# A transformer kernel whose first weights are loaded ahead of the norm's vectors, with the norm's gain and bias moved behind the transpose

## The reference

```python
def _layer_norm(x, g, b):
    mu = jnp.mean(x, axis=-1, keepdims=True)
    var = jnp.mean(jnp.square(x - mu), axis=-1, keepdims=True)
    return (x - mu) * lax.rsqrt(var + LN_EPS) * g + b

x = _layer_norm(x, ln_in_g, ln_in_b)
for l in range(DEPTH):
    mix = _mixer(x, w_in[l], b_f[l], w_pa[l], w_pb[l], w_pc[l], w_o[l])
    x = _layer_norm(DN_ALPHA * x + mix, ln1_g[l], ln1_b[l])
    ffn = _swiglu(x, w_gate[l], w_up[l], w_down[l])
    x = _layer_norm(DN_ALPHA * x + ffn, ln2_g[l], ln2_b[l])
```

## Time and profile before

| | |
|---|---|
| time, median of 3 runs | 873.25 us (873.02 to 873.25) |
| profiled execution | 873.52 us, of which the span is 871.7 us |
| TensorE busy (PE) | 840.5 us, 96% of the span |
| VectorE (DVE) | 513.3 us, 59% |
| ScalarE (ACT) | 400.1 us, 46% |
| GpSimd (POOL) | 56.7 us, 7% |
| bytes by DMA | 149.35 MB, mean 171 GB/s |
| first transpose on TensorE | 11.64 us |
| first weight pass on TensorE | 17.40 us |

### The profile page before, as it was taken

How to read it: one execution, slowest core, us unless ns; L and a number is a source line. 1 busy time by engine, 2 the same in 40 slices (tenths; PEclk the granted TensorE clock), 3 DMA queues, 4 the chain that set the end, 5 groups by cost and what they waited for, 6 DMA issues and landing times.

```text
span 871.7 us, 10732 instructions
## 1 busy us (share of the span) xinstructions
PE 840.5 (96%) x4216; PEld 695.9 (80%) x4216; DVE 513.3 (59%) x728; ACT 400.1 (46%) x536; POOL 56.7 (7%) x86
## 2 busy tenths in 40 slices
PE   3999999999999999999999999999999899999995
PEld 2888888888877888888878889888888688888884
DVE  7565564556796545445685656463778764555436
ACT  3476465543344344444336655554443453344430
POOL 0012331000000000000000324200000000000000
PEclk9999999999999999999999999999999999999998
DMA  9574433457636765664436443435654576656501
GB/s 324 160 257 164 133 119 116 141 181 229 193 104 244 232 194 183 193 203 149 154 108 225 144 159 106 142 103 181 243 177 144 192 246 203 189 183 193 193 0 49
DMA packets 93458, 149.35 MB, mean 171 GB/s; under 512 B 3424, under 2 KB 52832, under 8 KB 93408
## 3 DMA queue, kind: packets, MB, share of 16 engines
q1 hardware_dynamic: 93408, 148.66, 52.5%
HBM read 147.60 MB, written 1.05 MB: 171 GB/s over the span
## 4 chain that ended last, share of the span: by engine, by line
PE 92%; DVE 5%; DMA 1%; ACT 0%; issue 0%; SPq 0%; DVEq 0%
PE bank L1044 82%; PE bank L1059 3%; PE bank L1103 3%; PE bank L1135 2%; DVE w_lo L860 2%; PE bank L1123 1%; PE bank L1069 1%; DMA raw<-in_w_in 1%; DVE stats L977 1%; DVE x L1010 1%; DVE x L974 1%; DVE x L1007 1%; DVE act_lo L865 0%; DVE newton L994 0%; DVE rstd L999 0%
## 5 line engine op out<-in xcount | busy, mean ns | idle before, releaser
L860 DVE TENSOR_TENSOR w_lo<-raw,w_hi 128x2048 fp32r<-128x2048 f32 (+3 forms) x142 | 309.0, 2180 | 91.5 <-ACT w_hi L762 91.0
L1044 PE MATMUL bank<-w_hi,act_hi 128*128 128x512 f32 (+2 forms) x864 | 342.8, 397 | 3.3 <-DVE act_lo L865 3.3
L1044 PE MATMUL bank<-w_hi,act_lo 128*128 128x512 f32 (+2 forms) x864 | 333.3, 386 | 0.0
L1044 PE MATMUL bank<-w_lo,act_hi 128*128 128x512 f32 (+2 forms) x864 | 332.2, 384 | 0.0
L762 ACT CAST w_hi<-raw 128x2048 fp32r<-128x2048 f32 (+3 forms) x142 | 257.2, 1813 | 125.5 <-PE bank L1044 100.4
L1044 PEld LDWEIGHTS bank<-w_hi,act_hi 128*128 128x128 f32 x864 | 163.2, 189 | 33.2 <-DVE act_lo L865 3.7
L1044 PEld LDWEIGHTS bank<-w_hi,act_lo 128*128 128x128 f32 x864 | 162.8, 188 | 33.0
L1044 PEld LDWEIGHTS bank<-w_lo,act_hi 128*128 128x128 f32 x864 | 163.4, 189 | 28.8
L1044 PE MATMUL bank<-w_hi,y_hi 128*128 128x512 f32 x240 | 95.2, 397 | 0.0
L1044 PE MATMUL bank<-w_hi,y_lo 128*128 128x512 f32 x240 | 93.7, 390 | 0.0
L1044 PE MATMUL bank<-w_lo,y_hi 128*128 128x512 f32 x240 | 93.5, 390 | 0.0
(11 more groups left out here) (88 smaller groups left out, 551.3 us busy)
## 6 DMA issues: line engine op xcount, KB each, us to landing
raw<-in_w_in SPq DMA_DIRECT2D x48, 1024.0 KB, 5.2
raw<-in_w_gate SPq DMA_DIRECT2D x44, 512.0 KB, 4.0
raw<-in_w_up SPq DMA_DIRECT2D x44, 512.0 KB, 5.0
raw<-in_w_down SPq DMA_DIRECT2D x22, 1024.0 KB, 4.9
raw<-in_w_o SPq DMA_DIRECT2D x8, 1024.0 KB, 5.2
raw<-in_w_in SPq DMA_DIRECT2D x4, 768.0 KB, 4.4
raw<-in_w_pa SPq DMA_DIRECT2D x4, 768.0 KB, 4.4
raw<-in_w_pc SPq DMA_DIRECT2D x4, 768.0 KB, 4.4
```

Source lines behind the costliest of these rows:

```text
L860: dve.tensor_tensor(weights(w_lo, i, HI_SLOTS), weights(raw, i, RAW_SLOTS), weights(w_hi, i, HI_SLOTS).bitcast(F32), ALU.subtract).then_in ...
L1044: ins = pe.matmul(bank[use[0]][:, 0:width], a, w[:, k, c0:c0 + width], start=start and k == 0 and p == 0, stop=stop and k == nk - 1 and p ...
```

## The change

It concerns the input norm and the first pieces of layer 0.

- **Loads.** SyncE issues x, then piece 0, then the 64 KB identity and a new 8 KB array with gain and bias as columns (`norm_cols`, 128 x 2 x 8), then two more pieces. The broadcast rows of gain and bias are loaded behind the fifth piece, and the three table transfers (528, 131 and 6 KB) behind the seventh piece instead of the third.
- **Quarters.** The former piece 0 is two pieces of 128 x 1024 (two k blocks each) that share one slot. Pieces are so counted one higher from there on. The low part of the second quarter is made by GpSimd, not by VectorE.
- **Norm.** VectorE only computes (x - mean) * rstd, one operation per half, with no gain. The turn transposes that; then ScalarE applies gain and bias, which are now one value per partition: four operations of 128x128 from the bank into a part of `merged`, and the cast to act_hi and the subtraction to act_lo read it there. x for the residual gets its gain and bias later (step "affine"): two VectorE operations of 128x1024 per tile, behind column block 1 in the plan.
- **Idle passes.** TensorE starts with 48 matmuls of zeros (256 columns, into a bank that isn't in use), and does 16 more behind the first turn.
- **Order.** In layer 0 column block 0 is done for both tiles, then block 1. Splits of pieces 3 to 5 are planned behind block 0 of tile 0.

Everything else, the rest of layer 0 and layer 1, stays.

```diff
+ACT_SLOTS = [[0, 1, 2, 3], [4, 5, 6, 7]]
 HELD = 3
+WARM = (48, 16)
...
+        if layer == 0 and c == 0:
+            for quarter in range(2):
+                piece(("qkv", 0, 0, quarter), [(rows(w["w_in"], 2 * quarter, 2, c0, width), 0, width)], 2, width)
+        for half in range(layer == 0 and c == 0, 2):
             piece(("qkv", c, half), [(rows(w["w_in"], 4 * half, 4, c0, width), 0, width)], 4, width)
...
     statistics({t: None for t in range(TT)}, 1)
     scale(0)
     split_hi()
     split_lo()
-    turn_x(0, 0, 1)
     split_hi()
     split_lo()
+    plan.append(("warm", WARM[0]))
+    turn_x(0, 0)
+    plan.append(("warm", WARM[1]))
     scale(1)
-    for _ in range(HI_SLOTS - 2):
-        split_hi()
+    split_hi()
+    split_lo()
+    turn_x(0, 1)
 
     staged = [0]
     events = []
...
+        if layer == 0:
             for c in range(2):
...
+                for t in range(TT):
+                    if (c, t) == (0, 1):
+                        for _ in range(HI_SLOTS - 2):
+                            split_hi()
+                    use0 = bank(2 * c + t)
+                    for half in range(2):
+                        if (c, t, half) == (0, 0, 1):
+                            turn_x(1, 0, 1)
+                        qkv(c, t, (half,), use0, t == TT - 1, False)
+                    if c == 1:
+                        plan.append(("affine", t, turned[t, 1]))
...
-            sp.dma_start(tables[:, 0:P], d["tables"][:, 0:P]).then_inc(ident_loaded, 16)
-            load_gain_bias(0)
...
+                    if i == 1:
+                        sp.dma_start(tables[:, 0:P], d["tables"][:, 0:P]).then_inc(ident_loaded, 16)
+                        sp.dma_start(norm_cols[:, :, :].rearrange("p a k -> p (a k)"), d["norms"]
+                                     ).then_inc(norms_loaded, 16)
...
-                    if i == 2:
+                    if i == 4:
+                        load_gain_bias(0)
+                    if i == 6:
...
+            pool.wait_ge(hi_done, 2)
+            pool.tensor_tensor(weights(w_lo, 1, HI_SLOTS), weights(raw, 1, RAW_SLOTS),
+                               weights(w_hi, 1, HI_SLOTS).bitcast(F32), ALU.subtract).then_inc(lo_on_pool, 1)
...
+                    source_rows = bank[b]
+                    if src == "first":
+                        if idx == 1:
+                            act.wait_ge(norms_loaded, 16)
+                        source_rows = first_rows[dk // 4]
+                        if t:
+                            act.wait_ge(drained[first_use[dk][0]], first_use[dk][1])
+                        first_use[dk] = (b, n)
+                        for k in range(nk):
+                            ins = act.activation(source_rows[:, k * P:(k + 1) * P], bank[b][:, k * P:(k + 1) * P],
+                                                 ACT.Identity, bias=norm_cols[:, 1, dk + k:dk + k + 1],
+                                                 scale=norm_cols[:, 0, dk + k:dk + k + 1])
+                        link(ins)
                     act.copy(hi[dst][:, dk:dk + nk, t * P:(t + 1) * P],
-                             group_view(bank[b], nk, P)).then_inc(turn_hi, 1)
+                             group_view(source_rows, nk, P)).then_inc(turn_hi, 1)
...
-                if kind == "lo":
+                if kind == "lo" and step[1] != 1:
...
+                elif kind == "affine":
+                    _, t, (b, n) = step
+                    dve.wait_ge(gb_loaded, 32)
+                    dve.wait_ge(filled[b], n)
+                    link(dve.tensor_tensor(x[t][:, :], x[t][:, :], gain_bias[:, 0, :], ALU.mult))
+                    link(dve.tensor_tensor(x[t][:, :], x[t][:, :], gain_bias[:, 1, :], ALU.add))
+                elif kind == "scale" and step[2] <= TT:
+                    _, t, idx = step
+                    for nh in range(2):
+                        xh = x[t][:, nh * NW:(nh + 1) * NW]
+                        dve.tensor_scalar(xh, xh, mean_var[:, t, 0:1], rstd[:, t:t + 1], ALU.subtract,
+                                          ALU.mult).then_inc(x_ready, 1)
...
-            pe.wait_ge(ident_loaded, 16)
+            pe.wait_ge(logf_zeroed, 2)
             for step in PLAN:
                 kind = step[0]
+                if kind == "warm":
+                    for _ in range(step[1]):
+                        pe.matmul(bank[4][:, 0:SEQ], logf_hi[:, 0, :], logf_lo[:, :, :].rearrange("p t n -> p (t n)"),
+                                  start=True, stop=True)
+                    if step[1] == WARM[0]:
+                        pe.wait_ge(ident_loaded, 16)
                 if kind == "mm":
```

More of the change, by code:

```diff
@@ L328, in qkv @@
             for half in halves:
-                mm(at[("qkv", c, half)], t, ("act", 4 * half), [(use, 0, QKV[c][1], half == 0, half == 1)],
-                   frees, turned[t, half], (use,) if half else ())
+                if (layer, c, half) == (0, 0, 0):
+                    for quarter in range(2):
+                        mm(at[("qkv", 0, 0, quarter)], t, ("act", [2 * quarter, 2 * quarter + 1]),
+                           [(use, 0, QKV[0][1], quarter == 0, False)], frees, turned[t, 0])
+                else:
+                    mm(at[("qkv", c, half)], t, ("act", ACT_SLOTS[half]),
+                       [(use, 0, QKV[c][1], half == 0, half == 1)], frees, turned[t, half], (use,) if half else ())
                 if tick_too and not (half == 1):
@@ L430, in gate_up @@
         def gate_up(c, t, half, use, frees):
[L431 removed]
+            mm(at[("gu", c, half)], t, ("act", ACT_SLOTS[half]), [(use, 0, NW, half == 0, half == 1)],
                frees, turned[t, half], (use,) if half else ())
@@ L546, in trunk @@
         tables = sb("tables", [P, TABLE_COLS])
+        norm_cols = sb("norm_cols", [P, 2, KT])
+        first_rows = [merged[1][:, j * NW:(j + 1) * NW] for j in range(2)]
         cum_row = sb("cum_row", [P, SEQ], F32R)
@@ L864, in _ @@
                     dve.wait_ge(turn_hi, idx)
-                    dve.tensor_tensor(lo[dst][:, dk:dk + nk, t * P:(t + 1) * P], group_view(bank[b], nk, P),
+                    full = group_view(first_rows[dk // 4] if src == "first" else bank[b], nk, P)
+                    dve.tensor_tensor(lo[dst][:, dk:dk + nk, t * P:(t + 1) * P], full,
                                       hi[dst][:, dk:dk + nk, t * P:(t + 1) * P].bitcast(F32),
@@ L1181 @@
     arrays["in_tables"] = constant_tables()
+    arrays["in_norms"] = np.ascontiguousarray(np.concatenate(
+        [np.asarray(inputs[name]).reshape(KT, P).T for name in ("ln_in_g", "ln_in_b")], axis=1))
     for name, a in arrays.items():
```

82 lines of the change are left out of this document (44 added, 38 removed).

## The result

The changed kernel takes **876.06 us** (median of 10 runs, 873.80 to 879.22); the kernel before, beside it on the same chip, 873.42 (10 runs, 873.02 to 874.09). The ratio is 1.0032, with a 95% interval of 1.0020 to 1.0044: 0.3% slower, where 870.3 was forecast, and above the forecast's range of 867.2 to 873.4. The profiled execution took 878.12 us, span 876.3, one of the slower ones; where it matters, its times are read against a second profile of the same kernel (after_again, span 872.2). Of the before kernel the profiled execution took 873.52, span 871.7.

A forecast was written before the change was run, and what follows sets the result against it. TensorE's weight passes were taken as the bound from 17.40 us, with VectorE's chain then allowing the forget sum at 54.9. Gain 57.8 - 54.9 = 2.9, so 873.25 - 2.9 = 870.3 us; range 867.2 to 873.4.

The forecast's parts named there:

- From 17.40 TensorE's weight passes hold it, almost unbroken.: Chain of waits in the kernel before: TensorE's weight passes bound it from 17.40 us on.
- The rest of the kernel is the same and shifts with it: Everything behind the forget gate's sum moves along unchanged; sum at 54.9 instead of 57.8, so 2.9 us gained.
- Scaling at 9.95, GpSimd beside it.: Input norm: VectorE's first scaling starts at 9.95 and runs beside GpSimd's low part, which starts at 9.65.
- GpSimd's piece gets in front of the scaling: Rival, chance 0.24: GpSimd holds the scaling until 12.25, x comes 2.3 later, gain falls to 0.6: 872.6 us.
- Piece 7 lands 5.9 after its issue.: Weight transfer of piece 7: issued by SyncE at 28.6, lands 5.9 us later at 34.5.
- the tables blocking SyncE's issue: Rival, chance 0.11: table transfers ahead of piece 7 delay its issue by 4.1 us, giving 874.5 us.
- VectorE: 15.3 from the cast to the forget step, 3.1 to logf_lo.: VectorE behind piece 7's cast: 15.6 us of work less 0.3 to the forget gate at 51.8, sum possible 3.1 later.
- ScalarE's turn 2.1: ScalarE per half tile: four gain-and-bias ACTIVATEs taken as 1.5 us, plus a cast of 0.59, 2.1 instead of 0.59.
- Scaling 0.69 each: VectorE's scaling of x: one operation of 128x512 per half, taken as 0.69 us.
- GpSimd 1.2 to 2.6: GpSimd's low part of the second quarter: at most 2.6 us, with 1.21, half the VectorE split, as floor.
- Split 3 from 24.0: VectorE's split of piece 3 runs from 24.0 to 26.3, 0.8 us before TensorE wants it at 27.1.
- This rival has no time of its own: Rival of idle passes failing to keep the clock fast: costs 0.3 us, covered by the new forget-gate wait; no separate time.

The follow-up runs named there:

- before_idle_passes: The kernel before with idle passes on TensorE alone, 72 at the start and 26 behind the first tile's transposes: 873.42 us, ratio 0.9999.
- low_on_vector: The changed kernel with the low part of the second quarter on VectorE instead of GpSimd: 873.86 us, ratio 1.0004.
- low_and_gate: low_on_vector with 26 idle passes of 256 columns on TensorE in its wait for the forget sum: 873.66 us, ratio 1.0005.
- tables_mid: low_on_vector with the three table transfers issued behind piece 5 instead of behind piece 6: 872.16 us, ratio 0.9989.
- low_and_affine: low_on_vector with both tiles' affine moved ahead of the split of piece 7, into VectorE's idle stretch: 871.38 us, repeated 871.29.
- gate_passes: The changed kernel with 26 idle passes of 256 columns on TensorE ahead of its wait for log f: 876.37 us, ratio 1.0038.
- sum_ahead: low_and_affine with layer 0's cumulative sums ahead of a cast on ScalarE and ahead of a split on VectorE: 871.41 us.
- affine_behind_gate: The changed kernel with both tiles' affine on VectorE behind the forget step instead of ahead of it: 878.63 us, ratio 1.0067.
- no_idle_passes: The changed kernel without its 48 and 16 idle passes: 876.89 us, ratio 1.0048.
- tables_late: low_on_vector with the three table transfers issued behind piece 7 instead of behind piece 6: 872.89 us, ratio 0.9995.
- gpsimd_behind_scaling: The changed kernel with one more wait: GpSimd starts its low part only after VectorE has scaled the first tile: 874.50 us, ratio 1.0015.
- after: The first profile of the changed kernel, unedited; that execution took 878.12 us, span 876.3.
- all_three: sum_ahead with the three table transfers behind piece 7: 872.77 us.
- low_affine_tables: low_and_affine with the three table transfers behind piece 5: 871.46 us.

## Why the prediction was wrong

One relation of the profiles settles most of it. From the end of logf_lo on VectorE to the first scores on TensorE (times and span are of the profiled execution, the median is of all runs):

| kernel | logf_lo ends | scores start | block of 24 | span | median |
|---|---|---|---|---|---|
| before | 56.16 | 61.09 | 69.15 | 871.7 | 873.42 |
| before_idle_passes | 55.98 | 60.90 | 68.95 | 871.5 | 873.42 |
| changed | 59.14 | 65.37 | 73.45 | 876.3 | 876.06 |
| changed, second profile | 56.37 | 61.40 | 69.49 | 872.2 | 876.21 |
| low_on_vector | 56.19 | 61.10 | 69.18 | 872.0 | 873.86 |
| low_and_gate | 55.83 | 60.76 | 68.84 | 871.7 | 873.66 |
| tables_mid | 54.13 | 59.06 | 68.69 | 871.4 | 872.16 |
| low_and_affine | 53.82 | 58.75 | 66.83 | 869.6 | 871.38 |

Scores start 4.9 to 5.0 behind logf_lo in every row but one (the changed kernel's first profile, 6.2, where the clock was slow for twelve passes), whether TensorE waits or not; the block of 24 follows 8.1 later (9.6 in tables_mid, where the twelve passes behind the scores took 4.43); the span ends 802.5 to 802.9 behind that. The kernel before is on this line too. What fills the 4.9 is the cast, the split and the row in the chain of gate_passes above. Off the line are kernels that change what lies between: sum_ahead, with the row ahead of cast and split, 3.5, and affine_behind_gate, with four more operations there, 8.4; and no_idle_passes, 6.6, where TensorE was last.

Now the steps, in the order of the prediction.

- *"From 17.40 TensorE's weight passes hold it, almost unbroken."* **This failed first.** In before the row of sums ended at 60.95 and the scores started at 61.09, 0.14 later. In low_and_gate, where TensorE demonstrably waits for the row, the distance is the same 0.14 (60.62 to 60.76). So at this place TensorE had no slack to give: its passes and the row came in together, and the chain of waits named only TensorE. before_idle_passes took 2.5 us off TensorE's first 24 passes and gained nothing. I had looked for the next tight place, found 1.65 of slack at the sum, and stopped there; the next one, 3 us further, had none.
- *"The rest of the kernel is the same and shifts with it"*, the gain of 2.9 read at the sum. By the relation above logf_lo at 54.9 gives 54.9 - 56.16 = -1.3, so even with each other number right the time would have been 872, not 870.3. That the sum itself moved 2.9 was of no use.
- *Scaling at 9.95, GpSimd beside it.* The rival "GpSimd's piece gets in front of the scaling" (0.24) happened, with its 2.3 (12.20 instead of 9.95), but not in every execution. Its price in the median is 2.35 (876.21 to 873.86). I had the rule, and drew from it the wrong order: I let VectorE's scaling start 0.3 behind GpSimd and run. Even 128x1 operations with two tensor inputs were held, 2.41 for 0.23. What the Trainium skill says (SBUF — State Buffer, SBUF: two separate sides), that whoever starts first has the shared ports for its whole instruction and the other fully blocks, fits all three profiles: the held operation ended 0.09, 1.08 and 0.55 behind the end of GpSimd's (12.08, 13.23 and 14.36).
- *Piece 7 lands 5.9 after its issue.* It took 7.24 (6.6 to 7.5 in the other profiles with this order of transfers, 8.3 in no_idle_passes). It went out behind the tables; tables_mid shows the same piece 5.1 after the split that lets it go (28.82 to 33.97), and 1.7 less time. The rival had the tables blocking SyncE's issue; they took 0.51, 0.43 and 0.43. It was the bytes.
- *VectorE: 15.3 from the cast to the forget step, 3.1 to logf_lo.* Cast at 38.98, its end 40.9, forget at 56.04: 15.1, and 3.1. Right, as was the cause, the affine in that chain: moving it into the idle time gains 2.5 (873.86 to 871.3). I had named 34.5 as the landing of a piece that VectorE waits for and did not ask what else could stand there.
- *ScalarE's turn 2.1*: 1.51 + 0.62. *Scaling 0.69 each*: 0.50. *GpSimd 1.2 to 2.6*: 2.34. *Split 3 from 24.0*: 24.34 in low_on_vector, with the first weight pass at 14.25 for 14.2. So the beginning was right but for GpSimd, in part by luck: VectorE makes both quarters there and ends at 13.23, where I had GpSimd and then VectorE end at 13.46. In the changed kernel it stood at 27.19, 3.2 late: 2.25 is the hold, and with x late TensorE had been idle for 3.0, so the 16 idle passes ran at half clock (3.18) in front of the second transposes.
- *"This rival has no time of its own"* (the idle passes and the clock): right for the median, as gate_passes and low_and_gate show, and wrong for the slowest group: the clock fell in the new wait, which I had not thought of. There it cost 65.4 - 64.1 = 1.3.

Together: 870.3, plus 1.6 for reading the gain at the sum instead of at the scores, plus 1.3 for logf_lo at 56.2 instead of 54.9 without GpSimd in the way (low_on_vector; nearly all of it piece 7's transfer), plus 2.35 for GpSimd, make 875.55, of 876.06. 0.2 of the rest is the kernel before itself, 873.42 here and 873.25 there.

Open is why the quarters land about 1 us earlier in some executions than in others, which sets the order of GpSimd and VectorE, and what parts the upper groups of times. Not tried is to give GpSimd a share of the work where VectorE idles, at 35 to 40.9.

## What to carry to other kernels

A chain of waits names who came last, not by how much: before pricing a gain on it, write down the second arrival at each of the next meeting points, and take the smallest slack as the most that can be gained by speeding up the one named. An in-order engine that waits for a transfer is the place for work that nobody waits for; the same four operations cost 2.5 us behind that wait, and in front of it 1.15 of VectorE's wait was still left. A transfer that is moved needs an idle stretch of the DMA, since between two pieces of a serial chain its bytes are on the path.

## What the runs showed of the hardware

- When a GpSimd subtraction of 128x1024 begins close to a VectorE operation, the order of the two can differ from one execution to the next: GpSimd at 9.74 and the scaling held to 12.20 in one profile, the scaling at 9.98 and GpSimd at 10.67 in the other. The times of this one program lay in three groups, 0.6% apart: 873.8 to 875.0, 876.0 to 876.9, 877.9 to 879.6. One more wait (gpsimd_behind_scaling) made it 874.1 to 875.9.
- The hold reached operations of one column: 2.41 us for a pair that takes 0.23. The GpSimd subtraction took 2.34 when it was first, and 3.23 when VectorE's quarter was.
- TensorE idle for 3.0 us came back at a granted clock of 0.50, at once or within 1.5 us, and had 1.00 again 3 to 6 us after its return (after, after_again, low_on_vector); 26 idle passes in that wait kept it at 1.00. The length of the idle stretch alone does not decide: 3.2 us of it in all_three were followed by 1.00 throughout, and after a wait of 1.4 the clock stayed at 1.00 in low_and_affine and fell to 0.50 in tables_mid and low_affine_tables. In no_idle_passes a wait of 1.7 us was followed by 0.50 from 46 to 58 us.
- The record of the granted clock reads 1.00 from 18 to 22 us in the kernel before, while its passes start 0.42 apart. For the first passes it is the distance of the starts that tells the level.
- A 1 MB transfer landed 5.1 us after its issue with 268 KB issued 2.2 us ahead of it (tables_mid), 6.6 to 7.5 with 0.67 MB of tables there as well (8.3 in no_idle_passes), and 9.2 behind the tables and another 1 MB piece (tables_late).
